# Two-layer hybrid backbone on one core: earlier data for two attention stages, context work amid the key tiles, last totals by halves, last down products in two steps

## What is computed

```python
def attend(q, k, v):          # (B, Nq, Hkv, G, dh)
    s = jnp.einsum('bqkgd,bskd->bkgqs', q, k) * (q.shape[-1] ** -0.5)
    p = jax.nn.softmax(s.astype(jnp.float32), axis=-1)
    return jnp.einsum('bkgqs,bskd->bqkgd', p, v)
...
def mixing_sublayer(...):
    hg_l, hg_c = hgrn2_mix(...)                       # 4 heads, gated recurrence
    gq_l, gq_c = gqa_mix(...)                         # 6 query heads, 2 key heads, rms-norm and rotary
    na_l, na_c = na_mix(...)                          # 6 heads, 8 x 16 neighbourhood + all context keys
    y_lat = jnp.concatenate([hg_l, gq_l, na_l], axis=-1) @ w_out
...
def swiglu(h, w1, w2):
    gate, up = jnp.split(h @ w1, 2, axis=-1)
    return (jax.nn.silu(gate) * up) @ w2
```

## Time and profile before

| | us |
|---|---|
| median of 3 runs | 4114.62 (4111.85 to 4121.70) |
| the profiled execution | 4113.32, span 4111.9 |
| mean granted clock of TensorE, share of full | 0.948 |

### The profile page before, as it was taken

How to read it: one execution, slowest core, us unless ns; L and a number is a source line. 1 busy time by engine, 2 the same in 40 slices (tenths; PEclk the granted TensorE clock), 3 DMA queues, 4 the chain that set the end, 5 groups by cost and what they waited for, 6 DMA issues and landing times. The chain is left out here.

```text
span 4111.9 us, 52262 instructions
## 1 busy us (share of the span) xinstructions
PE 3703.2 (90%) x22354; PEld 2987.7 (73%) x22354; DVE 1768.0 (43%) x1933; ACT 1065.8 (26%) x1473; POOL 208.3 (5%) x118
## 2 busy tenths in 40 slices
PE   7999568979899999999998999468978989999998
PEld 5887446458777888888886888346467768888886
DVE  3122757566434323333326212757656243333334
ACT  2000422546324111111114100422456151111113
POOL 0000003013000000000000000002021000000000
PEclk8999779989999999999999999679989989999999
DMA  8423541031431111111113632340042211111111
GB/s 249 107 80 115 193 137 37 7 106 49 158 98 47 31 31 46 39 38 31 35 31 123 143 97 91 143 153 11 11 118 82 95 47 40 53 46 46 48 44 46
DMA packets 294825, 318.74 MB, mean 78 GB/s; under 512 B 42399, under 2 KB 261131, under 8 KB 294411
## 3 DMA queue, kind: packets, MB, share of 16 engines
q1 hardware_dynamic: 269034, 267.43, 21.8%
q0 software_dynamic: 6912, 30.15, 2.4%
q10 hardware_dynamic: 18720, 18.88, 1.4%
HBM read 247.78 MB, written 71.59 MB: 78 GB/s over the span
## 5 line engine op out<-in xcount | busy, mean ns | idle before, releaser
L566 PE MATMUL psum<-h_hi,lead_hi 128*128 128x512 f32 (+1 forms) x1432 | 392.8, 370 | 12.7 <-DVE h_lo L1090 7.4
L566 PE MATMUL psum<-h_lo,lead_hi 128*128 128x512 f32 (+1 forms) x1432 | 391.4, 369 | 0.0
L566 PE MATMUL psum<-h_hi,lead_lo 128*128 128x512 f32 (+1 forms) x1432 | 390.7, 368 | 0.0
L1213 DVE SCALAR_TENSOR_TENSOR y<-psum,mods,y 128x1024 f32<-128x1024 f32 (+1 forms) x264 | 260.4, 1014 | 258.2 <-PE psum L566 257.3
L566 PEld LDWEIGHTS psum<-h_hi,lead_hi 128*128 128x128 f32 x1432 | 251.9, 190 | 60.6 <-issue 8.2
L1178 ACT CAST f_whi<-lead_raw 128x1024 fp32r<-128x1024 f32 x44 | 46.3, 1053 | 941.1 <-PE psum L566 930.7
L566 PEld LDWEIGHTS psum<-h_lo,lead_hi 128*128 128x128 f32 x1432 | 251.9, 190 | 46.1
L566 PEld LDWEIGHTS psum<-h_hi,lead_lo 128*128 128x128 f32 x1432 | 251.4, 190 | 46.1
L566 PE MATMUL psum<-h_hi,w_hi 128*128 128x512 f32 (+1 forms) x856 | 230.6, 372 | 38.5 <-DVE w_lo L827 26.2
L716 DVE COPY lin_stage<-psum 128x1280 f32<-128x1280 f32 (+1 forms) x48 | 68.9, 1436 | 447.7 <-PE psum L566 447.7
L1226 DVE TENSOR_TENSOR f_hid<-f_silu,psum 128x1280 f32<-128x1280 f32 (+1 forms) x44 | 59.6, 1355 | 458.1 <-PE psum L566 333.5
(11 more groups left out here) (280 smaller groups left out, 6159.2 us busy)
## 6 DMA issues: line engine op xcount, KB each, us to landing
lead_raw<-in_w_ffn_in SPq DMA_DIRECT2D x88, 512.0 KB, 6.2
ada_w<-in_w_ada SPq DMA_DIRECT2D x30, 1024.0 KB, 11.3
lead_raw<-in_w_in SPq DMA_DIRECT2D x48, 512.0 KB, 5.3
proj_cm<-lin_stage POOLq DMA_DIRECT2D x38, 640.0 KB, 4.2
f_raw<-in_w_ffn_out SPq DMA_DIRECT2D x44, 512.0 KB, 3.7
ada_w<-in_w_ada ACTq DMA_DIRECT2D x18, 1024.0 KB, 5.8
na_qk<-proj_cm SPq DMA_DIRECT2D x48, 320.0 KB, 7.7
hg_pj<-proj_cm SPq DMA_DIRECT2D x20, 640.0 KB, 9.5
```

The source lines that it names most:

```text
L566: ins = nc.tensor.matmul(out[:, t0:t0 + tn], w, h[:, t0:t0 + tn], start=start and n == 0, stop=stop and n == 2)
L1213: ins = nc.vector.scalar_tensor_tensor(out=y[:, o, t0:t1], in0=sets(o + 1)[:, t0:t1], scalar=gate[:, o, m:m + 1], in1=y[:, o, t0:t1], op0= ...
```

## The change

Six things are changed.

1. A class `Staged` holds the keys, three slots for queries (later the values of neighbourhood attention), and the query and key buffers of neighbourhood attention across the stages. `gqa_prepare` copies the rotated keys and the queries of heads 0 to 2 inside SBUF, from `gq_pj` to where `gqa_attention` reads them, and stores only blocks 1 and 2. It ends when those copies have landed. The constant rows of `key_lo_ones` (64x2560) are filled by GpSimd.
2. In layer 0 the context scores of a pair stand behind the turned scores of key tile 5, the context products behind those of tile 6, each ahead of the products of the tile before; VectorE's part stands behind tile 7's additions. Their PSUM slots are renumbered accordingly.
3. The last pair's totals go to PSUM banks that no pair uses then, half by half. VectorE inverts each half straight from PSUM and multiplies by halves; ScalarE's copy is gone.
4. SyncE issues the loads of heads 0 and 1 and of the values for neighbourhood attention inside `gqa_attention`, the heads behind the last query load, the values when the last query's low part is done. In `na_attention` it starts with two bias loads.
5. In tiles that `differ` the scores of the context keys stand in columns 0 to 255 and the local ones from 256 on; the pieces are 256, 320 and 256 columns wide, not 512, 64 and 256. The other tiles stay.
6. The last down products begin with the first block's half of output 1, then of output 0; behind the wait for the second block's low parts come the second halves of outputs 0 and 1, then the others as before.

```diff
--- before.py
+++ after.py
@@ swiglu, TensorE
-                def down(p, last=False):
+                def down(p):
...
+                def last_down(p):
+                    def part(o, q):
+                        cols = slice(o * P, (o + 1) * P)
+                        return three_products(nc, sets(o + 1), chunks, d_hi[:, q, cols], d_lo[:, q, cols], u_hi[:, q], u_lo[:, q], q == 0, q == 1)
+                    pe.wait_ge(s_lo[2].h, s_lo[2].at(1) + p * 2)
+                    pe.wait_ge(s_ulo.h, s_ulo.at(1) + p * 2)
+                    pe.wait_ge(s_silu.h, s_silu.at(2) + p * 2)
+                    part(1, 0)
+                    pe.wait_ge(s_h.h, s_h.at(2) + p * 2)
+                    part(0, 0)
+                    pe.wait_ge(s_lo[2].h, s_lo[2].at(2) + p * 2)
+                    pe.wait_ge(s_ulo.h, s_ulo.at(2) + p * 2)
+                    for o in range(2):
+                        part(o, 1).then_inc(s_out.h, 1)
+                    for o in range(2, KB):
+                        pe.wait_ge(s_acc.h, s_acc.at(o - 1) + p * KB)
+                        part(o, 0)
+                        part(o, 1).then_inc(s_out.h, 1)
...
@@ na_tiles
-        pieces = [(0, k0 * GRID_W, 512)] + [(512, (k0 + NA_KH) * GRID_W, GRID_W)] * differ + [(local, SEQ, CTX)]
...
+        own, far = (CTX, 0) if differ else (0, local)
+        first = 512 - own
+        pieces = [(own, k0 * GRID_W, first)] + [(512, k0 * GRID_W + first, local - first)] * differ + [(far, SEQ, CTX)]
...
@@ na_attention, SyncE
-                head(0)
-                for i in range(3):
-                    sp.dma_start(vraw[:, i], k.pj_dram[:, V_BLOCK + i]).then_inc(s_vl.h, 16)
                 bias(0)
-                for h in range(1, HEADS):
-                    head(h)
+                bias(1)
+                for h in range(2, HEADS):
+                    sp.wait_ge(s_lo.h, s_lo.at(h - 1))
+                    staged.load_head(sp, h)
                     bias(h)
@@ class Staged
+        self.keys = k.sb(stack, "key_raw", [P, 2, NT])
+        self.three = k.sb(stack, "queries_or_values", [P, 3, NT])
+        self.heads = k.sb(stack, "na_qk", [P, 2, 2, NT])
...
+    def load_keys(self, sp, block):
+        for v in range(2):
+            for part in range(2):
+                sp.dma_start(self.keys[part * HD:(part + 1) * HD, v], block[v * HD:(v + 1) * HD]).then_inc(self.s_k[v].h, 16)
+
+    def load_query(self, sp, h, block, tokens):
+        for part in range(2):
+            sp.dma_start(self.three[part * HD:(part + 1) * HD, h % 3, 0:tokens], block[(h % 2) * HD:(h % 2 + 1) * HD, 0:tokens]).then_inc(self.s_q[h % 3].h, 16)
...
@@ gqa_attention, slots
-        if ctx:
-            slot_of[("ctx_score", b)] = len(slot_of)
-            slot_of[("ctx_out", b)] = len(slot_of)
-    slot_of[("total", PAIRS - 1)] = len(slot_of)
+            if ctx and kt == CTX_KT:
+                slot_of[("ctx_score", b)] = len(slot_of)
+            if ctx and kt == CTX_KT + 1:
+                slot_of[("ctx_out", b)] = len(slot_of)
@@ gqa_attention, SyncE
-                keys(0)
-                queries(0)
-                keys(1)
-                for h in range(1, HEADS):
-                    queries(h)
+                for h in range(3, HEADS):
+                    sp.wait_ge(s_qlo.h, s_qlo.at(h - 2))
+                    staged.load_query(sp, h, k.pj_dram[:, GQ_COL // P + h // 2], tokens)
+                staged.load_head(sp, 0)
+                staged.load_head(sp, 1)
+                sp.wait_ge(s_qlo.h, s_qlo.at(HEADS))
+                staged.load_values(sp)
@@ gqa_attention, GpSimd
+                nc.gpsimd.memset(kx[HD:P].bitcast(F32), 1.0).then_inc(s_kone.h, 1)
                 pool.wait_ge(s_khi.h, s_khi.at(2))
@@ gqa_attention, TensorE
+                def last_totals():
+                    pe.wait_ge(s_add.h, s_add.at(2 * PAIRS * (TT - 1)))
+                    pe.wait_ge(s_o.h, s_o.at(PAIRS - 1))
+                    for c, (t0, tn) in enumerate(lat_chunks):
+                        for half in range(2):
+                            ins = nc.tensor.matmul(last_tot[half * HD:(half + 1) * HD, c], ones[:], acc[:, half, t0:t0 + tn], start=True, stop=True)
+                        ins.then_inc(s_half.h, 1)
...
@@ gqa_attention, VectorE
-                nc.vector.memset(kx[HD:P].bitcast(F32), 1.0).then_inc(s_one.h, 1)
                 nc.vector.memset(qm[HD:P, 0].bitcast(F32), 0.0).then_inc(s_qz.h, 1)
...
+                def last_finish():
+                    b = PAIRS - 1
+                    dve.wait_ge(s_o.h, s_o.at(b))
+                    for c in range(2):
+                        dve.wait_ge(s_half.h, s_half.at(c + 1))
+                        nc.vector.reciprocal(inv[:, c * 512:(c + 1) * 512], last_tot[:, c]).then_inc(s_inv.h, 1)
...
@@ gqa_prepare, SyncE
-                    sp.dma_start(k.pj_dram[:, GQ_COL // P + i], pj[:, i]).then_inc(s_kd.h, 16)
-                after(sp, s_kd, N * 16)
+                    if i == 3:
+                        staged.load_keys(sp, pj[:, 3])
+                    for h in range(2 * i, 2 * i + 2):
+                        if h < 3:
+                            staged.load_query(sp, h, pj[:, i], n_tok)
+                    if i in (1, 2):
+                        sp.dma_start(k.pj_dram[:, GQ_COL // P + i], pj[:, i]).then_inc(s_kd.h, 16)
+                after(sp, s_kd, 2 * 16)
+                for v in range(2):
+                    after(sp, staged.s_k[v], 32)
+                for h in range(3):
+                    after(sp, staged.s_q[h], 32)
```

149 lines of the change are left out of this document (81 added, 68 removed).

## The result

| | before | changed |
|---|---|---|
| median | 4113.62 us (4 runs, one more than ahead of the prediction, 4111.85 to 4121.70) | 4076.36 us (4 runs, 4070.68 to 4085.07) |
| span of the profiled execution | 4111.9 us | 4071.6 us |
| mean granted clock | 0.948 | 0.953 |

The changed kernel is faster: ratio 0.9907, 95% interval 0.9884 to 0.9931, so the gain is 37 us by the medians and 40.3 by the two profiled spans. The forecast was 4067 with a range of 4053 to 4083. The sign and the range hold, and some 10 of the 47 us forecast are missing. The table takes the two traces apart. Each row is the time from one event to the next, layer 0 and layer 1.

The account below looks back on a forecast made before the run. TensorE, busy 90%, was taken as the bound, its idle time mostly at stage edges. Terms −11.6 + 1.2 + 1.7 − 3.8 − 18 − 6.3 − 10.6 = −47.4 gave a median of 4067 us, range 4053 to 4083.

Parts of the forecast that it names:

- The start: Start of grouped-query attention: data already there when the stage begins, first product 6.0 us earlier in layer 0, 5.6 in layer 1.
- I take 0 and keep +1 per layer: End of the prepare stage: copies land at 606 to 610, stage ends at 609.2, so no cost charged, +1 us kept per layer.
- rival (d): Prepare stage waits for the copies, so data comes no earlier: 4 us late in each layer, 4075 us; chance 0.07.
- (e): Rival: ten copies inside SBUF run one after another, each in 7.8 us, slower than before, 4187 us; chance 0.02.
- GpSimd against VectorE: First pass of grouped-query attention: small VectorE step waits for GpSimd's, +2.2 us in layer 0, 1.0 regained in layer 1.
- Context work: Layer 0, three pairs: context work amid key tiles waits 0.29 us for a PSUM slot, twice per pair, +1.7 us.
- The last totals: End of the pairs' stage: inverting and multiplying by halves straight from PSUM ends 1.9 us earlier per layer, −3.8 in all.
- The start of neighbourhood attention: Early loads bring the first score 10.2 us sooner; 1.2 taken off for TensorE's lower clock, −9 per layer, −18.
- rival (b): Bias load takes 16.5 us and decides the start of neighbourhood attention: 18 us less gain, 4085 us; chance 0.08.
- The pieces: Neighbourhood attention, 48 tiles spanning two starts: 0.165 us saved each, ten counted as swallowed by waits for ScalarE, −6.3 us.
- The last down: Last down products: early first halves save 5.3 us per layer, clock taken as kept behind the 2.0 us wait, −10.6.
- rival (a): Clock falls in both last down waits and once more at a start behind a stop: 4073 us; chance 0.22.

Follow-up runs that it names:

- in the second: Second profile: the changed kernel run once more without any edit, beside other kernels; 4080.50 us, ratio 0.9913 to the kernel before.

## Why the prediction was right, and where not

The sign and most of the size were right because the two large terms, the start and neighbourhood attention, were read off stages where TensorE demonstrably waits for data that could have been there, with durations of the same instructions. Three terms were not as forecast: a cost put at nothing, a cost too small, and a gain too large.

- **The start** (−11.6): the term itself was right to half a us, −12.1. The step that failed is the cost line beside it: "I take 0 and keep +1 per layer". I had priced a copy by its landing time alone, 4.0 to 7.8 us, as if ten could land side by side. Those were landing times of a queue, in which each transfer took the DMA engines 1.4 us. The copies landed by 602.8, 38.3 us behind the first square, and by the forecast's clock that is 608.3, within its 606 to 610. What it left out are the two stores behind them: they took 6.3 to 7.7 us in place of 2.9 to 4.0. The cost was +6.8 in the profiled pair and 6.2 in the means of all kernels. The rival (d) with its 4 us in each layer was nearest, held at 0.07, though the stage waits for the stores and not for the copies. In (e) the copies ran one after another, and so they did, but at 1.4 us each and not at 7.8.
- **GpSimd against VectorE** (+1.2): the mechanism and the place were right, the size not. In layer 1 the small step took 1.49 us, not 2.27, so −0.8 where I had let 1.0 go. In layer 0 the cast cost 3.3, 0.4 over my upper bound and 1.1 over the term, because the fill behind GpSimd's subtraction counted too, and some 0.6 came on top behind the wait, at the lower clock. The term's own working had a slip: 630.65 is the cast's start of before, 636.70, less 6.05; the subtraction of the earlier trace rows would have come at 630.93, for +2.0 and not +2.2. The first pass lost 6.4 in all; the other 2.9 are the turns of the maxima at the lower clock, for which the prediction has no term; 0.4 in layer 1 has no cause that I found.
- **Context work** (+1.7): 0.27 to 0.29 us at each of six places, as charged. What I had not seen is that this move is a condition of the gain at the last totals; the two terms are not independent.
- **The last totals** (−3.8): −2.0 in layer 1. In layer 0 −2.0 as well, given the context work's place.
- **The start of neighbourhood attention** (−18): −20.7, of which the runs show 1.6 to 3.0 given back behind the first score, as the forecast's 2.4 had it. The bias landed in 6.0 us at most, so the rival (b) is out.
- **The pieces** (−6.3): −6.3. The gain of a tile, 1.00 to 0.84 us, was read from rows; that 1.4 of 48 times 0.16 were swallowed agrees with the "ten" only by luck, since no run shows which tiles gained nothing.
- **The last down** (−10.6): −8.1 in the profiled pair and −7.9 in the mean of ten kernels. Two things were too large. The gain with the clock kept is 9.5 and not 10.6. And "I take the majority", four of six stops, was the wrong step: the clock was kept in eight of twenty cases, which takes another 1.6. In one kernel of ten it was kept in both layers, as forecast, in three it fell in both, as in the rival (a), and in six in one layer of the two.

The sum of the stretches, −33.4, stands against −37 by the medians and −40.3 by the profiled pair. The 4 to 7 us between them lie in unchanged code and in the spread between executions shown above; that they bring the measured time nearer to the forecast is in part luck. Added up by stretches the change is worth 33.4 us in the first profile and 33.9 in the second, of the 47 forecast.

## What to carry to other kernels

When a load is replaced by a copy in the stage before, add up what all transfers in that stretch take of the DMA engines, the stores behind them included: a landing time that grows from one transfer to the next is that of a queue, and its steps are the price (1.4 us for 320 KB here). And copy only what the next stage needs first: six copies kept the whole gain at the first product and their last store landed 0.9 us later than without copies, ten paid 3.1 us a layer for nothing more. Where GpSimd and VectorE both work on SBUF, a tiny VectorE step on the critical path can cost a whole GpSimd instruction; if GpSimd has slack, let it wait for the step, and the cost no longer depends on hundredths of a microsecond. When an end is shortened, look at the queue of the engine that closes it: the freed time may be held by another step of that same engine.

## What the runs showed of the hardware

- A copy inside SBUF of 64 rows of 5120 bytes landed in 3.4 to 6.7 us, and ten of them took the DMA engines from a share of 0.33 to over 1.0 at 231 to 243 GB/s. Loads of the same 64 rows from memory had 242 GB/s at a share of 1.04 (before, 612 to 617), while the loads of 128 partitions, 512 to 1024 KB each, had 403 GB/s at 1.03 (before, 570 to 580). So the difference goes with the shape of the transfer; the copy's staying inside SBUF adds nothing that shows.
- A fill by GpSimd of 64x2560 (606.26 to 608.49) did not hold up VectorE's subtraction of two SBUF operands beside it (607.93, 1.48 us, as without it).
- A VectorE cast of 128x10 that was issued 0.5 us into a GpSimd subtraction ended with the GpSimd fill behind it, 3.54 us after its start (3.49 to 3.83 in five traces); casts in the way of a fill alone took 1.0 us (fill 1.16). A VectorE subtraction in the same place ended with GpSimd's subtraction, and was not held by the fill (2.89 us, ending at 637.49, while the fill had started at 637.40). The rule of the Trainium skill named in the prediction ("SBUF — State Buffer", section "Who interferes with whom") makes the same difference: two SBUF inputs contend only with a GpSimd instruction that reads SBUF, VectorE's two-port modes, which a cast can enter, with any. The traces agree, if the cast runs in such a mode, which no row tells.
- The clock: behind a wait of 1.8 to 2.0 us in the last down it was at the lower level in 12 of 20 cases. At the turns of the maxima in layer 0 the wait is 0.93 us in every kernel, and the 20 turns took 2.34 us in eight kernels and 3.7 to 4.0 in five. In layer 1 the wait is 2.0 us, and the 16 turns took 1.91 us in seven kernels and 2.7 to 3.5 in six. No row of these runs says what decides it.
